# Two more gate/up pairs by seven half products, and the sums of weights for the first of them made among the norms

## The reference

```python
m = (jax.nn.sigmoid(gate_a) * (o_a @ w_branch_sparse[l])
     + jax.nn.sigmoid(gate_b) * (o_b @ w_branch_sb[l]))
x = x + rmsnorm(m @ w_out[l], g_post_mix[l])
h = rmsnorm(x, g_pre_ffn[l])
g, u = jnp.split(h @ w_gate_up[l], 2, axis=-1)
x = x + rmsnorm((jax.nn.silu(g) * u) @ w_down[l], g_post_ffn[l])
```

## Time and profile before

| what | us |
|---|---|
| median of 3 runs | 746.82 (746.49 to 747.61) |
| profiled execution, its own time | 747.47 |
| its span in the trace | 745.4 |
| TensorE busy | 738.6 |
| VectorE busy | 571.3 |
| ScalarE busy | 437.9 |
| GpSimd busy | 258.5 |
| first two pairs' tiles, second halves | 418.39 to 429.91 |
| two plain pairs | 429.91 to 451.7 |
| 18 sevens | 451.81 to 633.51 |

### The profile page before, as it was taken

The page is one execution under the profiler, slowest core; times in us unless marked ns, Lnnn a source line. Parts: engine busy times, 40 slices in busy tenths (PEclk is TensorE's granted clock), DMA queues, the critical chain, the costliest instruction groups (busy, mean ns, idle before and its releaser), DMA issues.

```text
span 745.4 us, 11725 instructions
## 1 busy us (share of the span) xinstructions
PE 738.6 (99%) x4232; PEld 650.6 (87%) x4232; DVE 571.3 (77%) x814; ACT 437.9 (59%) x701; POOL 258.5 (35%) x200
## 2 busy tenths in 40 slices
PE   9999999999999999999999999999999999999997
PEld 7788888888888888888888989999999999788885
DVE  4979989977666657358998677778877776985787
ACT  5763177777768576753575554455554554765664
POOL 6837265975777869311100520000000000043101
PEclk9999999999999999999999999999999999999999
DMA  9662433212304223179960025333333334899914
GB/s 336 184 174 61 153 114 112 58 57 67 104 17 119 71 66 112 57 219 285 254 188 1 1 76 151 113 92 90 100 113 113 113 113 156 338 183 205 211 23 113
DMA packets 111489, 95.22 MB, mean 128 GB/s; under 512 B 3665, under 2 KB 91737, under 8 KB 111449
## 3 DMA queue, kind: packets, MB, share of 16 engines
q1 hardware_dynamic: 104888, 78.96, 34.2%
q0 software_dynamic: 6368, 15.73, 11.4%
q10 hardware_dynamic: 192, 0.01, 0.0%
HBM read 84.97 MB, written 4.73 MB: 120 GB/s over the span
## 4 chain that ended last, share of the span: by engine, by line
PE 96%; DVE 2%; ACT 1%; issue 1%; POOL 0%; POOLq 0%; DVEq 0%
PE ps L674 12%; PE ps L676 12%; PE ps L675 12%; PE ps L1069 11%; PE ps L1015 8%; PE ps L1017 8%; PE ps L1016 8%; PE ps L695 6%; PE ps L937 4%; PE ps L736 3%; PE ps L894 3%; PE ps L883 2%; PE ps L957 1%; PE ps L866 1%; PE ps L868 1%
## 5 line engine op out<-in xcount | busy, mean ns | idle before, releaser
L674 PE MATMUL ps<-h_hi,w_hi 128*128 128x512 f32 (+1 forms) x320 | 123.7, 387 | 0.0
L676 PE MATMUL ps<-h_hi,w_lo 128*128 128x512 f32 (+1 forms) x320 | 121.9, 381 | 0.0
L675 PE MATMUL ps<-h_lo,w_hi 128*128 128x512 f32 (+1 forms) x320 | 121.8, 381 | 0.0
L1829 POOL DMA_DIRECT2D w_a<-in_w_down x12 | 15.3, 1532 | 229.2 <-DVE xd_lo L2384 229.2
L1764 POOL TENSOR_TENSOR w_lo<-raw,w_hi 128x1024 fp32r<-128x1024 f32 x30 | 78.3, 2612 | 30.5 <-ACT w_hi L1265 30.1
L676 PEld LDWEIGHTS ps<-h_hi,w_lo 128*128 128x128 f32 x320 | 60.2, 188 | 11.4
L675 PEld LDWEIGHTS ps<-h_lo,w_hi 128*128 128x128 f32 x320 | 60.4, 189 | 9.7
L674 PEld LDWEIGHTS ps<-h_hi,w_hi 128*128 128x128 f32 x320 | 60.3, 189 | 9.8
L2379 DVE TENSOR_TENSOR wr_lo<-w_a,wr_hi 128x1536 fp32r<-128x1536 f32 (+1 forms) x28 | 45.5, 1625 | 21.4 <-ACT wr_hi L1573 21.4
L1017 PE MATMUL ps<-t_hi,sum_lo 128*128 128x256 f32 x216 | 61.2, 283 | 0.0
L1016 PE MATMUL ps<-t_lo,sum_hi 128*128 128x256 f32 x216 | 61.2, 283 | 0.0
(11 more groups left out here) (335 smaller groups left out, 2163.5 us busy)
## 6 DMA issues: line engine op xcount, KB each, us to landing
raw<-in_w_in SPq DMA_DIRECT2D x40, 512.0 KB, 4.5
raw<-in_w_gate_up SPq DMA_DIRECT2D x26, 512.0 KB, 3.8
raw<-in_w_gate_up SPq DMA_DIRECT2D x36, 256.0 KB, 4.2
w_a<-in_w_down SPq DMA_DIRECT2D x9, 768.0 KB, 7.0
w_a<-in_w_down POOLq DMA_DIRECT2D x9, 768.0 KB, 10.7
s<-in_w_out SPq DMA_DIRECT2D x3, 768.0 KB, 8.1
w_a<-w_a POOLq DMA_DIRECT2D x3, 768.0 KB, 13.1
x_t<-in_first SPq DMA_DIRECT2D x8, 256.0 KB, 6.7
```

Of the source, the lines that this page charges most:

```text
L674: mm(acc, whi_c, a_hi_, start=first, stop=False)
L675: mm(acc, whi_c, a_lo_, start=False, stop=False)
L676: return mm(acc, wlo_c, a_hi_, start=False, stop=last)
```

## The change

Two pairs more go by seven half products and two less as plain pairs (PLAIN = 2, SEVENS = 20). The first seven follows the second halves of the first tiles directly. On VectorE its four sums of weights move among the norms: the first two behind the fourth `sum_x1`, the other two between rest_turned(2) and rest_turned(3). quarters_rest(0, 0) goes behind rest_turned(3), ahead of the t sums, and both `up` products go behind the t rests. ScalarE rounds the quarters between second_norm(2) and second_norm(3), and the sums behind round_turned(3). TensorE's first seven waits for the four t rests one by one. GpSimd's four splits go. Buffers change places so that the first seven's parts can be written that early; the first seven's sums get a place of their own (`first_sums`), in the region of `act`. One more small matmul stands behind the first seven.

```diff
-SEVENS = FC - 4
+SEVENS = FC - 2
-PLAIN = 4
+PLAIN = 2
...
-        up(1)
...
-        pe.wait_ge(t_hi_done, 5)
-        pe.wait_ge(t_done, OUT_T + 8)
+        pe.wait_ge(t_hi_done, 1)
+        pe.wait_ge(t_done, OUT_T + 3)
 
         mm(bank(5, HALF), h_hi[:, 0, 0:P], h_hi[:, 0, 0:HALF], start=True, stop=True).then_inc(product_done, 1)
-        seven(0, 0)
+        seven(0, 0, lambda n: pe.wait_ge(t_done, OUT_T + 5 + n))
         pe.wait_ge(act_done, 2 + PLAIN)
+        mm(bank(1, HALF), h_hi[:, 0, 0:P], h_hi[:, 0, 0:HALF], start=True, stop=True)
...
         first_norm(3)
         second_norm(2)
+        sc.wait_ge(y_normed, TB)
+        quarters_hi(0, 0)
         second_norm(3)
         round_turned(2)
         nc.scalar.preload_act_table(ACT.Silu)
         round_turned(3)
+        sums_hi(0, 0, 0)
...
         sums_hi(0, 0, 1)
...
+        t_part_hi(0)
+        silu_plain(0)
+        for i in range(1, 4):
+            t_part_hi(i)
+        silu_plain(1)
...
-        gp.wait_ge(w_lo_done, T_UP + 4)
-        for d in range(T_UP // 2 + 2, T_DOWN // 2):
-            for u in range(2):
-                split(d, u)
...
+        def raw_sums(p, v):
+
+            ve.wait_ge(up_in, p * 48 + (OUT_IN + 48))
+            sum_of(p, v, 0, quarter(v, 3), quarter(v, 2))
+            sum_of(p, v, 2, quarter(v, 0), quarter(v, 3))
+
+        def second_sum(p, v):
+            sum_of(p, v, 1, sums_of(p, v, 0), quarter(v, 0), 1)
+
+        def third_sum(p, v):
+            sum_of(p, v, 3, sums_of(p, v, 1), quarter(v, 1), 3)
...
         sum_x1(3)
+        raw_sums(0, 0)
         second_norm(3)
         rest_turned(2)
+        second_sum(0, 0)
+        third_sum(0, 0)
         rest_turned(3)
...
+        quarters_rest(0, 0)
         ve.wait_ge(early_made, 2)
         ve.wait_ge(t_hi_done, 1)
         tt(t_plain(0), early[:, 0:KC // 2, :], late[:, :, :], sub).then_inc(t_done, 1)
...
+        t_rest(0, 0)
+        sums_rest(0, 0, 0)
+        t_rest(2, 1)
+        sums_rest(0, 0, 1)
+        t_rest(1, 2)
+        t_rest(3, 3)
         up(0)
+        up(1)
...
-        first_sums(0, 0)
-        second_sum(0, 0)
-        third_sum(0, 0)
-        quarters_rest(0, 0)
-        sums_rest(0, 0, 0)
-        sums_rest(0, 0, 1)
-        up(1)
-        ve.sem_inc(summed_up, 4)
```

More of the change, by code:

```diff
@@ L298, in build, with sums_of @@
         sums.append(sb(f"sums{n}", 4 * Q))
-    top[0] = sets_at
+    top[0] = zone1 + 4 * 2 * S
+    first_sums = sb("first_sums", 4 * Q)
+    def sums_of(p, v, i, n=1):
+        return (first_sums if isinstance(p, int) and p == 0 else sums[v])[:, i * Q:(i + n) * Q]
+    top[0] = sets_at + 4 * 6 * Q
     w_a11 = sb("w_a11", [PAIRED, 512])
@@ L303, in build @@
     for n in range(3):
+        if n == 1:
+            assert top[0] <= zone2 - 4 * HALF
+            top[0] = sets_at
         xd_hi.append(sb(f"xd_hi{n}", [GROUP, HALF], F32R))
@@ L308, in build @@
         x_fly.append(sb(f"x_fly{n}", [GROUP, HALF]))
-    assert top[0] <= zone2
+    assert top[0] <= sets_at + 4 * 6 * Q
     top[0] = 0
@@ L999, in _ @@
             first_part(T_UP, i, 2, 4)
-        def up(j):
-            for u in range(2):
-                for g in range(2):
-                    weights(T_UP + 4 * j + 2 * u + g)
-                    if g == 0:
-                        pe.wait_ge(act_done, 2 * j + u + 1)
-                    proj_part(bank(2 * u + g), g, 0, KC).then_inc(tile_done, 1)
-        up(1)
         def product(acc, hi, lo, first_col, b_hi, b_lo, first):
@@ L1025, in t_sum, with seven @@
             return t_hi[:, i, :, :], t_lo[:, i, :, :]
-        def seven(p, v):
+        def seven(p, v, t_rest=None):
             first_bank = 4 - 4 * v
@@ L1033, in seven @@
             pe.wait_ge(parts_lo_done, p * 3 + (OUT_PARTS + 1))
-            pe.wait_ge(act_done, p + (1 + PLAIN))
+            if not t_rest:
+                pe.wait_ge(act_done, p + (1 + PLAIN))
             product(m, q_hi_, q_lo_, 0, *h_quarter(0, 0), True).then_inc(product_done, 1)
@@ L1457, in second_norm, with quarters_hi, sums_hi @@
             root(2, t)
+        def quarters_hi(p, v):
+            sc.wait_ge(up_in, p * 48 + (OUT_IN + 48))
+            run(quart_hi[v][:, 0:2 * Q], raw[:, 2 * v, :], ACT.Copy)
+            run(quart_hi[v][:, 2 * Q:3 * Q], raw[:, 2 * v + 1, 0:Q], ACT.Copy).then_inc(parts_hi_done, 1)
+        def sums_hi(p, v, n):
+            sc.wait_ge(sum_made, p * 4 + (n + 3))
+            run(sum_hi[v][:, 2 * Q * n:2 * Q * (n + 1)], sums_of(p, v, 2 * n, 2), ACT.Copy).then_inc(parts_hi_done, 1)
         first_norm(0)
@@ L2213, in second_norm, with quarter, sum_of @@
             norm_x1(t)
+        def quarter(v, n):
+            return raw[:, 2 * v + n // 2, n % 2 * Q:(n % 2 + 1) * Q]
+        def sum_of(p, v, i, x_, y_, made=None):
+            if made:
+                ve.wait_ge(sum_made, p * 4 + made)
+            tt(sums_of(p, v, i), x_, y_, ALU.add).then_inc(sum_made, 1)
+        def raw_sums(p, v):
[6 more added lines that the diff above has]
+            sum_of(p, v, 3, sums_of(p, v, 1), quarter(v, 1), 3)
         out_sum(0)
@@ L2249, in _, with quarters_rest, sums_rest @@
         late_down = ps[:, 5:8:2, :].rearrange("p t (c n) -> p c t n", n=P)
+        def quarters_rest(p, v):
+            ve.wait_ge(parts_hi_done, p * 3 + (OUT_PARTS + 1))
+            both = raw[:, 2 * v:2 * v + 2, :].rearrange("p u n -> p (u n)")
+            tt(quart_lo[v][:, :], both[:, 0:3 * Q], quart_hi[v][:, :], sub).then_inc(parts_lo_done, 1)
+        def sums_rest(p, v, n):
+            ve.wait_ge(sum_made, p * 4 + 4)
+            ve.wait_ge(parts_hi_done, p * 3 + (OUT_PARTS + n + 2))
+            part = slice(2 * Q * n, 2 * Q * (n + 1))
+            tt(sum_lo[v][:, part], sums_of(p, v, 2 * n, 2), sum_hi[v][:, part], sub).then_inc(parts_lo_done, 1)
+        quarters_rest(0, 0)
+        ve.wait_ge(early_made, 2)
+        ve.wait_ge(t_hi_done, 1)
         tt(t_plain(0), early[:, 0:KC // 2, :], late[:, :, :], sub).then_inc(t_done, 1)
```

102 lines of the change are left out of this document (27 added, 75 removed).

## The result

The changed kernel takes 750.63 us, median of 5 executions (750.05 to 751.62). The kernel before, run beside it on the same chip, takes 747.32 (746.49 to 747.61). The ratio is 1.0048, interval [1.0037, 1.0059]: 3.6 us slower, between 2.8 and 4.4. Run again on another chip, the same kernel took 750.00 against 746.93, ratio 1.0044 [1.0031, 1.0057]. The forecast was slower at 749.1, 2.25 us above the median of the kernel before. The sign and the main place were right, and the loss came out larger: 3.31 us by the medians of the first set and 3.07 by those of the second; the time is 1.5 us above the forecast.

The account below looks back on a forecast made before the run. TensorE, busy 99% of the span, was taken to bound the kernel. 2.48 + 0.62 + 0.62 - 1.47 = +2.25 us on the median of 746.82 gave 749.07, stated as 749.1; range 746.7 to 750.9.

Parts of the forecast that it names:

- "two cost 20.19", gain 1.47: TensorE: two sevens at 10.094 us replace two plain pairs of 21.78, plus a 0.12 matmul; saves 1.47 us.
- "TensorE wants all four blocks at 418.39 and gets them at 420.87": 2.48: Before the tiles' second halves, TensorE stands still 2.48 us because GpSimd holds VectorE's sums and the last h_lo is late.
- The order in which the two engines are served: Near 414 to 420 us, GpSimd's two early sums and VectorE's third and fourth sums alternate; the fourth ends at 419.68.
- (a): Rival: VectorE is served twice running, only the third sum held; 2.70 us lost, +1.2 net, 748.0; chance 0.13.
- (b): Rival: sums fit their gap, only the chain behind counts; 0.91 (or 1.57) lost, -0.6 to +0.1 net; chance 0.14.
- "VectorE's window starts 2.80 us into the seven", then 0.62 and 0.62: First seven: VectorE's late window makes TensorE's fifth and seventh products wait 0.62 us each.
- Rival (c): VectorE's chain is hidden too, needing 1.6 us less than the best of (b); gain stands whole, 745.3; chance 0.05.
- "The down stage keeps its order and waits [...] I take it at nothing, between -0.3 and +0.3, its wait of 0.2 us being all that shows.": Down stage: only places in SBUF change, so its effect is nothing, between -0.3 and +0.3 us.
- Rival (d), the clock: Standing still 2.5 us returns TensorE to 1.2 GHz, a loss of 2.7 partly hidden; +3.7 net, 750.5; chance 0.13.

Follow-up runs that it names:

- best2: Changed kernel with the edits of early_moved and tail_first, and the first window reordered so bank-freeing work goes first: 745.73 us against 747.21, ratio 0.9978.
- early_moved: Changed kernel with GpSimd's two early sums moved, one behind the second h_lo, one behind VectorE's fourth sum: 747.97 us against 747.00, ratio 1.0012.
- sums_behind: Changed kernel with VectorE's third and fourth sums of weights behind the last h_lo instead of ahead of it: 749.68 us, ratio 1.0032 to before.
- second trace: The changed kernel run again with nothing edited, for another trace: 750.00 us, ratio 1.0044 to the kernel before.
- filled: Changed kernel with 20 TensorE matmuls of 256 columns in the stop before the last h_lo: 749.68 us, ratio 1.0037 to before.
- tail_first: Changed kernel with up_2 and the first x rest ahead of the first w_down rest in the last seven: 749.67 us against 747.21, ratio 1.0032.
- gap_25_again: Kernel before with 2.88 us more unread VectorE work ahead of the last h_lo, run once more: ratio 1.0042.

## Why the prediction was right or wrong

**"two cost 20.19", gain 1.47.** Right in sum. A seven is 10.08, not 10.094; the mean had the last seven's 0.26 us of waiting in it. The gain is 1.50 by that, and best2 shows it whole, at 1.48.

**"TensorE wants all four blocks at 418.39 and gets them at 420.87": 2.48.** Right, 2.49. The order in which the two engines are served was read from the earlier trace rows, and came out with deviations below 0.1 us, once the 0.34 us by which the trace runs earlier is taken off. The Trainium skill, page "SBUF — State Buffer", section "SBUF: two separate sides", has the lock, and the trace agrees (1.97 and 2.76 us for sums of 0.69); that the waiting engine comes in between two queued instructions of the other, only the rows show. Rivals (a) and (b) are out: the fourth sum was held too, and the h_lo was late. early_moved shows the cause by removing it. sums_behind and early_moved show one thing more: without the stop, the wait at the fifth product grows.

**"VectorE's window starts 2.80 us into the seven", then 0.62 and 0.62.** Right in place and sum: it starts 435.06 - 432.16 = 2.90 in. The first wait was larger (1.02), the second smaller (0.12). TensorE came 0.35 us earlier than in the sum (432.16 for 432.51). The copy for the fifth product came earlier too, its end at 438.60 for 438.85, but TensorE started only 0.34 behind it (438.94), where I had put 0.05, the figure of VectorE's signals; in early_moved and sums_behind it is 0.25. up_2 ended 0.40 earlier than in the sum (441.95 for 442.35). Together 1.14 instead of 1.24. Rival (c) is out. Its condition was worked out wrongly: to hide the chain, the best of (b), 0.91 lost, would have had to be 0.9 us shorter; 1.6 is (b)'s other case.

**What each start again costs.** It was not in the sum, that is, taken at nothing. In the second trace the restarts at the stop and at the fifth and seventh product cost 0.10, 0.07 and 0.10, together 0.27.

**"The down stage keeps its order and waits [...] I take it at nothing, between -0.3 and +0.3, its wait of 0.2 us being all that shows."** This step failed. The down stage itself did keep its time (111.80 to 111.98 us in all traces), but its first load is wanted one stage earlier: the seventh product of the last seven waits for up_2, which stands behind that load on VectorE. I had left this link out. The last seven went from 10.34 us to 10.59 in the first trace of the change, which is within the bound of 0.3, and to 10.98 in the second, which is not; in filled it took 11.93. tail_first shows the link by cutting it: 10.08. That the link was at its limit could be read: ScalarE waited for w_a in the kernel before, and the last of 18 sevens was longer than the others. I took the mean of all 18 and didn't look for one that differs. That the load would land later could not be read there, and why it does stays open.

**Rival (d), the clock, at "+3.7 net, 750.5".** It happens, but only in about half of the executions (six of ten of the change by the mean clock, one of two by the trace), at a price of 1.47 and not 2.7, of which 1.30 is hidden behind the waits of the first seven. Its time came close to the measured one by luck: the change is as slow in executions without it, for the restarts and the last seven. The Trainium skill, page "TensorE: Matmul & The Clock Gate", Part 1, has an idle engine fall back to the lower level; the runs agree for 2.3 to 2.4 us idle in part of the executions and never showed it for 1.24. Against it I had put that "the engine is busy to the last moment before and works on at once"; that was no reason.

**The sum.** 2.48 + 1.24 - 1.47 = 2.25 was forecast. Second trace: +0.01 at the stop, +0.27 restarts, -0.10 waits in the first seven, +0.64 in the last, -0.03 by the gain, which makes 3.04. First trace: +0.01 at the stop, +0.10 for its restart, +1.47 for the clock in place of the 1.24 of waits, +0.25 in the last seven, -0.03 by the gain, which makes 2.81. So two terms were missing that no rival had: the restarts and the last seven. The second set of executions has 3.07 by the medians, the first 3.31. Of the 1.56 us between 749.07 and 750.63, 0.56 (first trace, the clock included) to 0.79 (second) are in these sums, and 0.50 is the basis: three executions gave 746.82 for the kernel before, those run beside the change 747.32, and later sets of 15 to 21 had medians of 746.93 to 747.21. The 0.3 to 0.5 that is left no trace shows; the traced execution was the fastest of its five.

## What to carry to other kernels

When an engine that bounds the kernel is given its next stage sooner, cost the whole chain that its neighbours then have to finish by that point, and look for the instructions of VectorE and GpSimd that meet in SBUF on that chain; here GpSimd's first sum went 8.5 us ahead, its second stayed near 416 us but behind VectorE's sums; that held one other VectorE instruction for 0.75 us and was worth 2.07 us of TensorE's time. Remove the waits in a row, not one: with the stop of 2.59 us gone, the waits of the first seven grew from 1.30 to 1.82, until what freed the banks was put ahead of what was made for later. And look at the last turn of a loop by itself, since a mean over all turns hides a wait that is there in one.

## What the hardware showed that I had not expected

- Behind a stop of 2.3 to 2.4 us idle the clock went to half for 3.41 us (seen in one trace of the changed kernel, from 1.3 us after TensorE's restart; not in the five other traces with a stop of 2.3 to 2.5 us); by the mean clock of each execution this came in six of 11 executions of the kernel before with the longer stop and in six of ten of the changed kernel, and behind stops of 1.24 and 1.29 us in none of 11 each. What decides it from one execution to the next stays open.
- 42 matmuls of 4 columns, back to back for 4.6 us, counted as busy throughout, were followed by the same 3.41 us at half clock in the trace, and the mean clock was low in all five executions; 20 matmuls of 256 columns were not (five executions).
- A matmul of 4 columns, with weights of its own, takes 0.11 us from start to start here (42 in 4.61 us), one of 256 takes 0.12.
- The first spacing behind a wait is 0.22 us instead of 0.12 (0.19 at the fifth product), and this comes whole even where the wait itself is 0.01 us (the last seven of gap_25_again).
- Two GpSimd and two VectorE instructions, all with their inputs in SBUF, went in turn (GpSimd, VectorE, GpSimd, VectorE): VectorE's ended 0.55 and 0.54 us behind GpSimd's, in the trace of the change.
- The first w_down load landed 4.56 to 4.86 us after its issue in the six traces without a 16 KB instruction fetch in it, and 4.78 to 6.44 in the eight with one; cause open.
